# Rearranged heads in an encoder layer: map one is scaled earlier, products with v run their high passes first, GpSimd forms T1

## The chip, the core and the metric

The kernel runs on one core of a Trainium2 chip. Its engines work side by side and meet through semaphores: TensorE (PE: products, transposes), VectorE (DVE), ScalarE (ACT), GpSimd (POOL), and SyncE (SP), which issues most transfers. The metric is the time of one execution on the device in microseconds. The kernel before took 1401.86 us in the median of three runs (1399.14 to 1402.75).

## What is computed

One encoder layer for 1024 tokens of width 1024. Cut to what matters for the change, the token mixing is

```python
u = rmsnorm(h, norm_g[l, 0])
proj = u @ w_in            # q, k, v of 4 heads, inputs of a short convolution, gates
s1 = einsum('bhqd,bhkd->bhqk', q1b, k1) * scale + bias     # bias: ALiBi
s2 = einsum('bhqd,bhkd->bhqk', q2b, k2) * scale + bias
a = softmax(s1) - lam * softmax(s2)
o = einsum('bhqk,bhkv->bhqv', a, v)
o = rmsnorm(o, subln_g) * (1.0 - lam_init)
merged = g[:, :, 0] * y_conv + g[:, :, 1] * (o @ w_attn_out)
h = h + rmsnorm(merged @ w_o, norm_g[l, 1])
```

and after it comes an MLP with a squared ReLU of width 4096. A head has 64 columns for q1, q2, k1, k2 each and 128 for v.

## The kernel before

All products are made from operands split into a high and a low part (`_hi`, `_lo`): hi x hi, lo x hi and hi x lo, three passes for each of eight row tiles (`PASSES`), so 24 products of 128x128 by 128x512 for one unit. ScalarE writes the high part (a copy that rounds), VectorE the low part (the source less the high part).

The heads run as 4 x 8 **blocks** (i, n): head i, 128 query rows n. Every engine has its own list, written out by hand; all that joins them is semaphores. On TensorE block (i, n) is: `scores(i, n)`, both maps, 24 half-height products; one **unit** `filler(i, n)`, a product of 24 for another purpose; and `turn((i, "T", n - 1))`, eight transposes of the combined map of the block before. The fillers of head i are, for n = 0 to 7: v0, AV1 of the head before, v1, k0 and k1 of the next head, AV0 of this head, q0 and q1 of the next head. In head 3 the units at n = 3, 4, 6, 7 are gates (g0 to g3). AV is the product of the turned map (`at_hi`, `at_lo`) with v; AV0 takes the turned maps 0 to 3, AV1 those of 4 to 7. v is turned in the middle of unit n = 3 (`turn((i, "VT", 0))`). Units use two PSUM banks in turn, so one waits until the unit two before it is copied out.

For one block the other engines do this. VectorE: `maximum` for map two, then map one (bias added, the row maximum into `small`); ScalarE: `exponential` of each; VectorE: `weights`, the reciprocals of the sums and a weight for map two; GpSimd: `e1 * weight`, then `e0 + e1`; ScalarE between them: `first_scaled`, `e0` by its reciprocal. The sum is turned on TensorE one block later, and ScalarE and VectorE copy the turned tile into `at_hi` (`turned_hi`) and `at_lo` (`turned_lo`). Between these steps stand, at given n: the copies of q, k and v (`copy_hi`, `copy_lo`), the split of the next weight panel (`panel_hi`, `panel_lo`), and the norm of o: `av_copy`, `o_squares` (ScalarE), `o_squares_lo` (VectorE), `o_sum` (TensorE, two products with ones), `o_deviation` (ScalarE, a square root, with a load of its table before it and one of the exponential's behind it), `o_inverse` (VectorE, four reciprocals and the scaling).

`o_sum` is made inside an AV unit, halfway (`o_inside`), into the bank of the unit before; its values are read by `o_deviation`.

Behind the heads comes the GATE stage, a product in seven terms (X1, Y, X2, Z1, X3 and so on) on sums T1 to T4 of `act` halves, each split again. T1 is u12 - u11, 2048 elements in a partition, formed in three passes (`t_sum(GATE, 1, k)`, total `g_sum1`, hi and lo parts of both); T3 is formed in three passes within head 3 at n = 2, 4, 7; T2 needs T1, T4 needs T2. From there TensorE runs on through the branch products, w_o and the MLP.

Lines of before in the rows below: 927 the products of a unit, 974 the transposes of a turn, 1007 scores, 1067 GATE terms; 888 and 891 GpSimd's scale and sum; 1349 exponential, 1356 `first_scaled`, 1362 `turned_hi`; 1831 `turned_lo`, 1838 `panel_lo`, 1893 `copy_lo`, 1910 maximum, 1922 weights, 1946 and 1949 `o_inverse`, 1987 `t_sum`.

## Time and profile before

| | us |
|---|---|
| median of three runs | 1401.86 |
| the profiled execution | 1399.67 |
| its span, first to last instruction | 1397.8 |
| TensorE busy (97% of the span) | 1361.4 |
| VectorE busy (69%) | 965.6 |
| ScalarE busy (46%) | 643.9 |
| GpSimd busy (20%) | 284.5 |

Busy time counts the engines' own instructions; waiting and issuing transfers is not counted. Time and rows are all of this one execution. Matmuls overlap each other, so a mean duration is longer than the distance from one to the next. In the rows a number in square brackets is the idle time of the engine just before, with what ended it.

### The profile page before, as it was taken

The page shows a single profiled execution, that of the slowest core. Times are in us where ns is not written, and L with a number is a line of the kernel's source. Part 1 is how long each engine was busy: PE and PEld are TensorE (multiplying, and loading weights), DVE is VectorE, ACT ScalarE, POOL GpSimd, SP SyncE. Part 2 cuts the span into 40 slices and gives each one's busy share as a digit, 9 for nine tenths or more (in the row PEclk, how much of TensorE's full clock was granted, in tenths as well). Part 3 has the DMA queues.
Part 4 walks back from the last instruction along what each step waited for, and adds up shares of the span by engine and source line. Part 5 has one row for each costly group of instructions (what it writes and reads, how often), then busy time and mean ns, then how long its engine had stood idle before and what let it go on. Part 6 is the DMA issues. An engine that isn't in the chain of part 4 may idle for free.

```text
span 1397.8 us, 17130 instructions
## 1 busy us (share of the span) xinstructions
PE 1361.4 (97%) x6305; PEld 1113.8 (80%) x6305; DVE 965.6 (69%) x1423; ACT 643.9 (46%) x985; POOL 284.5 (20%) x136
## 2 busy tenths in 40 slices
PE   9999999998999999999999999999999999999998
PEld 7777767676788888888888888888888888888886
DVE  7567777777977754566556788766674787765676
ACT  7566776675622244521243453333332444444454
POOL 0465565664000000000000133333233100000000
PEclk9999999999999999999999999999999999999999
DMA  5110101001122233264642065444444974336343
GB/s 185 31 31 16 31 16 31 16 31 60 46 61 61 68 106 113 76 196 147 225 153 72 35 189 174 155 153 146 156 166 155 381 270 128 98 102 215 105 132 109
DMA packets 141656, 162.18 MB, mean 116 GB/s; under 512 B 6861, under 2 KB 88970, under 8 KB 141450
## 3 DMA queue, kind: packets, MB, share of 16 engines
q1 hardware_dynamic: 135568, 148.27, 33.0%
q10 hardware_dynamic: 6010, 12.88, 2.4%
q8 instruction: 48, 0.79, 0.2%
q14 instruction: 30, 0.25, 0.0%
HBM read 114.98 MB, written 46.14 MB: 115 GB/s over the span
## 4 chain that ended last, share of the span: by engine, by line
PE 83%; DVE 7%; issue 6%; ACT 4%; POOL 1%; ACTq 0%; DVEq 0%; POOLq 0%
PE psum L1067 35%; PE psum L1227 21%; PE psum L927 19%; PE psum L1204 3%; DVE dev L1946 1%; PE psum L1007 1%; DVE at_lo L1831 1%; ACT e L1349 1%; PE psum L974 1%; DVE g_sum L1987 1%; ACT at_hi L1362 1%; PE psum L936 1%; PE psum L1176 1%; ACT w_hi L1266 0%; ACT L1373 0%
## 5 line engine op out<-in xcount | busy, mean ns | idle before, releaser
L1227 PE MATMUL psum<-op 128*128 128x512 f32 x1344 | 305.1, 389 | 0.1
L1227 PEld LDWEIGHTS psum<-op 128*128 128x128 f32 x1344 | 252.2, 188 | 52.9 <-issue 0.5
L1693 ACT ACTIVATE op<-v 128x512 fp32r<-128x512 f32 x112 | 70.7, 632 | 151.0 <-PE psum L1227 147.9
L2403 DVE TENSOR_TENSOR op<-v,op 128x512 fp32r<-128x512 f32 x112 | 78.6, 702 | 88.3 <-ACT op L1693 88.3
L888 POOL TENSOR_SCALAR e<-e,small 128x1024 f32<-128x1024 f32 x32 | 95.1, 2973 | 140.1 <-DVE small L1924 140.1
L1349 ACT ACTIVATE e<-e,small 128x1024 f32<-128x1024 f32 x64 | 73.7, 1152 | 73.9 <-DVE small L1915 71.1
L927 PE MATMUL psum<-act_hi,w_hi 128*128 128x512 f32 x256 | 104.4, 408 | 0.9 <-DVE act_lo L1832 0.9
L927 PE MATMUL psum<-act_lo,w_hi 128*128 128x512 f32 x256 | 100.7, 393 | 0.0
L927 PE MATMUL psum<-act_hi,w_lo 128*128 128x512 f32 x256 | 100.7, 393 | 0.0
L1067 PE MATMUL psum<-act_hi,w_lo 128*128 128x512 f32 x256 | 99.6, 389 | 0.0
L1067 PE MATMUL psum<-act_hi,w_hi 128*128 128x512 f32 x256 | 99.6, 389 | 0.0
L1067 PE MATMUL psum<-act_lo,w_hi 128*128 128x512 f32 x256 | 99.6, 389 | 0.0
L894 POOL TENSOR_TENSOR staging<-w_raw 128x512 f32<-128x512 f32 x1 | 1.3, 1299 | 456.4 <-ACT w_raw L1630 456.4
L891 POOL TENSOR_TENSOR e<-e,e 128x1024 f32<-128x1024 f32 x32 | 81.6, 2551 | 18.1 <-ACT e L1356 16.7
L2406 DVE TENSOR_TENSOR op<-f_raw,op 128x512 fp32r<-128x512 f32 x112 | 77.7, 694 | 5.4 <-ACT op L1695 5.4
L1910 DVE CUSTOM_DVE_ANT_0 e<-psum,alibi 128x1024 f32<-128x1024 f32 x64 | 78.0, 1219 | 0.4 <-issue 0.3
L1695 ACT ACTIVATE op<-f_raw 128x512 fp32r<-128x512 f32 x112 | 69.0, 616 | 6.6 <-DMA f_raw<-f_scratch 6.6
L1438 ACT ACTIVATE prod<-psum 128x512 f32<-128x512 f32 x36 | 21.5, 597 | 104.9 <-PE psum L1067 80.3
L927 PEld LDWEIGHTS psum<-act_hi,w_hi 128*128 128x128 f32 x256 | 48.7, 190 | 20.2 <-issue 9.0
L927 PEld LDWEIGHTS psum<-act_hi,w_lo 128*128 128x128 f32 x256 | 48.5, 190 | 10.6
L1067 PEld LDWEIGHTS psum<-act_hi,w_hi 128*128 128x128 f32 x256 | 48.0, 188 | 10.0
L1067 PEld LDWEIGHTS psum<-act_hi,w_lo 128*128 128x128 f32 x256 | 48.1, 188 | 9.9
(271 smaller groups left out, 3158.0 us busy)
## 6 DMA issues: line engine op xcount, KB each, us to landing
f_raw<-f_scratch SPq DMA_DIRECT2D x112, 256.0 KB, 2.6
w_raw<-in_w_ff SPq DMA_DIRECT2D x32, 512.0 KB, 5.3
w_raw<-in_w_in SPq DMA_DIRECT2D x28, 512.0 KB, 4.5
f_scratch<-f_out SPq DMA_DIRECT2D x56, 256.0 KB, 2.3
v<-in_w_ff SPq DMA_DIRECT2D x12, 1024.0 KB, 7.0
gates_scratch<-staging ACTq DMA_DIRECT2D x32, 256.0 KB, 2.0
gate_in<-gates_scratch SPq DMA_DIRECT2D x16, 512.0 KB, 4.3
f_scratch<-staging SPq DMA_DIRECT2D x30, 256.0 KB, 2.2
```

Source lines behind the costliest of these rows:

```text
L888: nc.gpsimd.tensor_scalar(e[s][1][:], e[s][1][:], weight2[s], None, ALU.mult).then_inc(a_ready, 1)
L891: nc.gpsimd.tensor_tensor(e[s][0][:], e[s][0][:], e[s][1][:], ALU.add).then_inc(a_ready, 1)
L927: mm = nc.tensor.matmul(bank, stat(a, kt), moving(b, kt), start=(n == 0), stop=(n == len(terms) - 1))
L1067: mm = nc.tensor.matmul(bank, stat[a][:, kt], moving(b)[:, kt], start=(first and n == 0), stop=(last and n == len(terms) - 1), skip_group_ ...
L1204: mm = nc.tensor.matmul(bank, w_hl[panel % RING][a][:, kt], act_hl[b][:, kt, half_cols[h]], start=(kt == 0 and (a, b) == PASSES[0]), stop= ...
L1227: mm = nc.tensor.matmul(psum[:, (X_BANK, Z_BANK)[m % 2][t]], op[n % SLOTS][:, 2 + a, token_cols(t)], op[n % SLOTS][:, b], start=(m in (0, ...
L1349: nc.scalar.activation(e[s][c][:], e[s][c][:], ACT.Exp, scale=SCALE, bias=neg_max[s][:, c:c + 1], accum_out=exp_sum[s][:, c:c + 1]).then_i ...
L1693: nc.scalar.activation(op[n % SLOTS][:, 0], v_block[m][:, kt], ACT.Copy).then_inc(v_hi, 1)
L1695: nc.scalar.activation(op[n % SLOTS][:, 2], f_raw[:, n % SLOTS], ACT.Copy).then_inc(f_hi, 1)
L1910: vec.tensor_tensor_reduce(out=e[s][c][:], in0=psum[:, SB + 2 * c:SB + 2 * c + 2].rearrange("p b c -> p (b c)"), in1=table[:, start:start ...
L2403: vec.tensor_tensor(slot[:, 1], v_block[m][:, kt], slot[:, 0].bitcast(F32), ALU.subtract).then_inc(v_split, 1)
L2406: vec.tensor_tensor(slot[:, 3], f_raw[:, n % SLOTS], slot[:, 2].bitcast(F32), ALU.subtract).then_inc(f_split, 1)
```

## The change

It moves instructions and adds one small piece; no arithmetic is left out.

1. Scores of block (0,0) are issued in the middle of unit (0,q,1) instead of ahead of it.
2. A new function `av` makes the AV units: first all passes with `at_hi` (v high and v low, 16 products), then the eight with `at_lo`. It waits for `tb_hi` and for v's low part at the start, and for `tb_free` (`at_lo` written) only before the last eight.
3. `o_sum` is no longer made in AV units but in units n = 0 and n = 4 of the next head, for (3,0) in (3,7), by a table `O_IN`. `o_deviation` moves along to n = 0 and 4.
4. ScalarE: `first_scaled` stands first in a block, then `turned_hi`, then the copy. The first panel of a head is split at n = 2 instead of n = 0.
5. VectorE: `turned_lo` first; the low part of q or k behind the first maximum (n = 0, 4) or behind both; the reciprocals of o two by two, at the end of blocks 0 and 4 and ahead of the weights in blocks 1 and 5, the scaling behind these weights; the third panel at n = 6 instead of 5; the scaling of the bias table from n = 0 to n = 7.
6. GpSimd forms T1, three passes after its last sum of the heads; VectorE's three steps for it are gone. The tail of the heads on ScalarE and VectorE is ordered anew.

```diff
+O_IN = {filler(HEADS - 1, QB - 1): (HEADS - 1, 0)}
+for _i in range(1, HEADS):
+    O_IN[filler(_i, 0)] = (_i - 1, 0)
+    O_IN[filler(_i, 4)] = (_i - 1, 1)
...
+            pool.wait_ge(s_read, HEADS * QB)
+            for k in range(3):
+                pool.wait_ge(t_steps, GATE.t_sum_at(1) - 3 + k)
+                total = GATE.t_sums[1][:]
+                in0 = total if k else u_part(0, 1, 2).bitcast(F32)
+                in1 = (u_part(0, 1, 1), u_part(1, 1, 2), u_part(1, 1, 1))[k].bitcast(F32)
+                nc.gpsimd.tensor_tensor(total, in0, in1, ALU.add if k == 1 else ALU.subtract).then_inc(t_steps, 1)
...
+                def o_between():
+                    bank_read(BANKED[at - 1])
+                    o_sum(*O_IN[x])
...
+            def av(i, n):
+
+                at = BANK_AT[i, "AV", n]
+                if BANKED[at - 1] in O_IN:
+                    pe.wait_ge(o_read, half_at(*O_IN[BANKED[at - 1]]))
+                else:
+                    bank_read(BANKED[at - 2])
+                turned = TB_AT[i, "T", 4 * n + 3]
+                pe.wait_ge(tb_free, TB_AT[i, "VT", 0])
+                pe.wait_ge(tb_hi, turned)
+                terms = [(kt, a, 0) for kt in range(TT) for a in range(2)] + [(kt, 0, 1) for kt in range(TT)]
+                for k, (kt, a, b) in enumerate(terms):
+                    if k == 2 * TT:
+                        pe.wait_ge(tb_free, turned)
...
+                    if (i, n) == (0, 0):
+                        unit(x, (), lambda: scores(0, 0))
+                        continue
...
             def head(i):
                 for n in range(QB):
+                    if n > 0:
+                        first_scaled(i, n - 1)
+                    elif i > 0:
+                        first_scaled(i - 1, QB - 1)
+                    if n > 1:
+                        turned_hi((i, "T", n - 2))
...
-                        turned_lo((i, "T", n - 2))
-                    maximum(i, n, 1)
-                    maximum(i, n, 0)
...
+                    maximum(i, n, 1)
+                    if copied and n in (0, 4) and (i, n) != (0, 0):
+                        copy_lo(earlier)
+                    maximum(i, n, 0)
+                    if copied and n not in (0, 4):
+                        copy_lo(earlier)
...
+                    if n in (1, 5) and i > 0:
+                        for part in (2, 3):
+                            o_inverse(i - 1, n // 4, part)
...
+                    if n in (1, 5) and i > 0:
+                        o_scale(i - 1, n // 4)
+                    elif n in (0, 4) and i > 0:
+                        for part in range(2):
+                            o_inverse(i - 1, n // 4, part)
```

ScalarE from the panel split of block (1,3) to the exponentials of block (1,4), before: `e_0<-e_0` is the scaling of map one, `at_hi` the turned tile, `k_hi` the copy of k.

```order
L1266 ACTIVATE w_hi<-w_raw 128x1024
L1334 ACTIVATE k_hi<-psum 128x512
L1362 ACTIVATE at_hi<-psum 128x8x128
L1356 ACTIVATE e_0<-e_0,small 128x1024
L1349 ACTIVATE e_1,small<-e_1,small 128x1024
L1349 ACTIVATE e_0,small<-e_0,small 128x1024
```

The same place after, where the square root for o (`dev`) follows the exponentials:

```order
L1298 ACTIVATE w_hi<-w_raw 128x1024
L1388 ACTIVATE e_0<-e_0,small 128x1024
L1394 ACTIVATE at_hi<-psum 128x8x128
L1366 ACTIVATE k_hi<-psum 128x512
L1381 ACTIVATE e_1,small<-e_1,small 128x1024
L1381 ACTIVATE e_0,small<-e_0,small 128x1024
L1405 ACT_TABLE_LOAD
L1405 ACTIVATE dev<-psum,small 128x512
```

The scaling went from third to first behind the panel, the copy of k from first to third.

VectorE from the same panel to the second maximum of block (1,4), before: `small<-small 128x2` are the weights' reciprocals, `e_1` and `e_0` from psum the maxima.

```order
L1838 TENSOR_TENSOR w_lo<-w_raw,w_hi 128x1024
L1922 RECIPROCAL small<-small 128x2
L1924 TENSOR_SCALAR small<-small,par 128x1
L1893 TENSOR_TENSOR k_lo<-psum,k_hi 128x512
L1831 TENSOR_TENSOR at_lo<-psum,at_hi 128x8x128
L1907 MEMSET small 128x1
L1910 ISA e_1,small<-psum,alibi 128x1024
L1910 ISA small 128x1
L1915 TENSOR_SCALAR small<-small 128x1
```

and after:

```order
L1867 TENSOR_TENSOR w_lo<-w_raw,w_hi 128x1024
L1951 RECIPROCAL small<-small 128x2
L1953 TENSOR_SCALAR small<-small,par 128x1
L1860 TENSOR_TENSOR at_lo<-psum,at_hi 128x8x128
L1936 MEMSET small 128x1
L1939 ISA e_1,small<-psum,alibi 128x1024
L1939 ISA small 128x1
L1944 TENSOR_SCALAR small<-small 128x1
L1922 TENSOR_TENSOR k_lo<-psum,k_hi 128x512
```

The low part of k moved from ahead of the turned tile to behind the first maximum.

TensorE at the first AV unit, block (0,5), before: the last two passes of the scores, then the unit.

```order
L1007 MATMUL psum<-k_lo,q_hi 128x512 x4
L1007 MATMUL psum<-k_hi,q_lo 128x512 x4
L927 MATMUL psum<-at_hi,v_hi 128x512
L927 MATMUL psum<-at_lo,v_hi 128x512
L927 MATMUL psum<-at_hi,v_lo 128x512
```

and after, the end of the unit and what follows it:

```order
L1060 MATMUL psum<-at_hi,v_hi 128x512
L1060 MATMUL psum<-at_hi,v_lo 128x512
L1060 MATMUL psum<-at_lo,v_hi 128x512 x8
L982 MATMUL psum<-ident,e_0 128x128 x8
L1015 MATMUL psum<-k_hi,q_hi 128x512 x4
```

`at_lo` was read by the second product of the unit and is now read by its last eight.

## Rows read from the trace of the kernel before

**Rows 1.** The page, costliest groups: busy, mean ns, idle before.
```profile
L891 POOL TENSOR_TENSOR e<-e,e 128x1024 f32<-128x1024 f32 x32 | 81.6, 2551 | 18.1 <-ACT e L1356 16.7
```

**Rows 2.** TensorE's waits: engine, line, releaser, us in total, times, longest.
```profile
PE psum L927 <- DVE at_lo L1831: 11.1, 7, 2.9
PE psum L974 <- POOL e L891: 6.3, 4, 4.7
PE psum L1007 <- DVE small L1910: 3.2, 4, 0.8
PE psum L1007 <- DVE k_lo L1893: 2.8, 1, 2.8
```

**Rows 3.** Stretches: us, busy PE, PEld, DVE, ACT, POOL, clock, DMA share, GB/s.
```profile
104.42:178.21 73.79, 67.71 (x366) 52.66 (x365) 56.13 (x109) 50.47 (x66) 41.77 (x16) 1.00 0.08 22
178.21:252.24 74.03, 69.14 (x367) 53.86 (x366) 55.11 (x111) 51.75 (x69) 42.84 (x16) 0.98 0.08 22
252.24:338.24 86.00, 74.81 (x389) 58.20 (x388) 67.04 (x117) 58.61 (x76) 54.09 (x18) 0.98 0.12 36
...
37.98:41.39 3.41, 3.41 (x12) 2.25 (x9) 2.41 (x6) 0.95 (x1) 0.00 (x0) 0.50 0.55 156
```

**Rows 4.** TensorE in order of time: start, us, line, tiles, idle before.
```profile
36.83 0.73 PE L1007 MATMUL psum<-k_hi,q_hi 64*128 64x512 f32 x4 [2.82 <-DVE k_lo L1893]
...
88.14 0.73 PE L1007 MATMUL psum<-k_hi,q_hi 64*128 64x512 f32 x4
...
89.73 0.50 PE L927 MATMUL psum<-act_hi,w_hi 128*128 128x512 f32 x1
...
96.28 0.73 PE L1007 MATMUL psum<-k_hi,q_hi 64*128 64x512 f32 x4
...
115.77 0.47 PE L927 MATMUL psum<-at_hi,v_hi 128*128 128x512 f32 x1 [1.54 <-DVE at_lo L1831]
...
142.85 0.73 PE L1007 MATMUL psum<-k_hi,q_hi 64*128 64x512 f32 x4
...
338.24 1.91 PE L974 MATMUL psum<-ident,e 128*128 128x128 f32 x8 [4.74 <-POOL e L891]
...
377.22 0.47 PE L1067 MATMUL psum<-act_hi,g_S_hi 128*128 128x512 f32 x1 [1.25 <-issue]
```

**Rows 5.** VectorE in order of time: start, block (1,4), o's inverses, tail.
```profile
36.09 0.68 DVE L1893 TENSOR_TENSOR k_lo<-psum,k_hi 128x512 fp32r<-128x512 f32 x1
...
142.56 1.23 DVE L1838 TENSOR_TENSOR w_lo<-w_raw,w_hi 128x1024 fp32r<-128x1024 f32 x1 [0.85 <-ACT w_hi L1266]
143.71 0.16 DVE L1922 RECIPROCAL small<-small 128x2 f32<-128x2 f32 x1
...
144.03 0.68 DVE L1893 TENSOR_TENSOR k_lo<-psum,k_hi 128x512 fp32r<-128x512 f32 x1
144.63 1.21 DVE L1831 TENSOR_TENSOR at_lo<-psum,at_hi 128x1024 fp32r<-128x1024 f32 x1
...
149.84 0.17 DVE L1922 RECIPROCAL small<-small 128x2 f32<-128x2 f32 x1 [1.31 <-ACT e L1349]
...
311.17 1.71 DVE L1946 RECIPROCAL dev<-dev 128x128 f32<-128x128 f32 x2
312.91 2.10 DVE L1949 SCALAR_TENSOR_TENSOR o<-o,par,dev 128x512 f32<-128x512 f32 x1
...
353.79 0.75 DVE L1949 SCALAR_TENSOR_TENSOR o<-o,par,dev 128x512 f32<-128x512 f32 x1
...
355.06 2.28 DVE L1987 TENSOR_TENSOR g_sum<-act_hi,g_sum 128x2048 f32<-128x2048 f32 x1
```

**Rows 6.** ScalarE in order of time, block (1,4): the turned tile, the scaling.
```profile
142.96 1.03 ACT L1362 ACTIVATE at_hi<-psum 128x1024 fp32r<-128x1024 f32 x1
143.90 1.15 ACT L1356 ACTIVATE e<-e,small 128x1024 f32<-128x1024 f32 x1
```

**Rows 7.** GpSimd in order of time, block (3,7), beside a sum of VectorE.
```profile
329.08 4.82 POOL L888 TENSOR_SCALAR e<-e,small 128x1024 f32<-128x1024 f32 x1 [2.19 <-DVE small L1924]
```

More of the change, by code:

```diff
@@ L1026, in unit @@
                     pe.wait_ge(map1_read, HEADS * QB)
-                if kind == "AV":
-                    pe.wait_ge(tb_free, TB_AT[i, "T", 4 * n + 3])
-                    between = o_inside(x) and (lambda: (bank_read(before), o_sum(psum[:, 1 - at % 2], *o_inside(x))))
-                    product(unit_bank(x), lambda a, kt: v_hl[a][:, kt], lambda b, kt: at_hl[b][:, kt], range(TT), (),
-                            between).then_inc(proj_done, 1)
-                    return
+                def o_between():
+                    bank_read(BANKED[at - 1])
+                    o_sum(*O_IN[x])
                 panel = panel_of(x)
@@ L1055, in _ @@
             unit((HEADS, "g", 5))
-            unit((last, "AV", 1))
+            av(last, 1)
             unit((HEADS, "g", 6))
-            pe.wait_ge(o_read, half_at(last, 0))
-            o_sum(psum[:, 1 - BANK_AT[last, "AV", 1] % 2], last, 1)
+            bank_read((HEADS, "g", 3))
+            o_sum(last, 1)
             unit((HEADS, "g", 7))
@@ L1523, in _ @@
                 if p == GATE.first:
+                    t_hi_part(GATE, 4)
                     x_copy(GATE, 3, p)
@@ L2115, in _ @@
             panel_lo(P_BR - 1)
-            t_sum(GATE, 1, 0)
-            t_sum(GATE, 1, 1)
+            for part in range(2):
+                o_inverse(last, 0, part)
             turned_lo((last, "T", 7))
-            t_sum(GATE, 1, 2)
+            for part in range(2, 4):
+                o_inverse(last, 0, part)
+            o_scale(last, 0)
             t_lo(GATE, 3)
-            o_inverse(last, 0)
             av_copy(last, 1)
+            o_squares_lo(last, 1)
             t_sum(GATE, 2, 0)
-            o_squares_lo(last, 1)
             t_sum(GATE, 2, 1)
@@ L2184, in _ @@
                 if p == GATE.first + 2:
-                    o_inverse(HEADS - 1, 1)
-                if p == GATE.first:
-                    g_part_lo("W11", p + 1)
-                    g_part_lo("S4", p)
+                    for part in range(4):
+                        o_inverse(HEADS - 1, 1, part)
+                    o_scale(HEADS - 1, 1)
                 g_sum("S3", p + 1)
```

144 lines of the change are left out of this document (68 added, 76 removed).

## The prediction, made before the result was known

> **What bounds the kernel now.** I read the list of TensorE's waits first, then the busy time by head, then TensorE's own rows at the waits, and last one block's rows on VectorE and ScalarE. TensorE is the bound, and from 377 us on nothing makes it wait before the last microseconds. All that can be won lies ahead of that. The list [rows 2] shows which waits: 11.1 us in seven waits of the product with v for `at_lo`, 6.3 us in four waits of a turn for GpSimd's sum, 3.2 us of scores for a maximum, 2.8 us once for `k_lo`. The busy time by head [rows 3] says the same: 73.79 us with 67.71 busy, 74.03 with 69.14, 86.00 with 74.81. After an idle stretch of 2.8 us or more the granted clock is 0.50 for 3.41 us (1.2 instead of 2.4 GHz), which costs half of it, 1.7 us [rows 3]; the head of 74.03 us and the 86.00 have the other ones. After the 1.54 us at 115.77 it did not fall [rows 4]. A plain block lasts 8.14 us on TensorE (88.14 to 96.28), 1.59 of it scores [rows 4].
>
> **Part 1, the start.** Scores (0,0) wait 2.82 us for `k_lo`, which VectorE ends at 36.77 [rows 5], and the clock falls behind it [rows 3, 4]. After the change the first half of unit (0,q,1), 12 of 24 products or 2.8 us, stands ahead of them; TensorE is free from 34.0 and reaches the scores at about 36.7, when `k_lo` is done. Both costs go: 2.8 + 1.7 = 4.5, less 0.1 of rest: **-4.4 us**. The cover is those 12 products; they need only panel 1 and the copy of (0,q,0), both long there.
>
> **Part 2, what the product with v waits for.** It now needs `at_hi` at its start and `at_lo` 16 products (3.6 us) later. `at_lo` takes 1.21 us [rows 5], so that wait is covered. But `at_hi` comes later than before: ScalarE now scales map one (`e_0`, 1.15 us [rows 6]) ahead of it, and that waits for the weights of the block before. This closes a loop that was open: weights(n-1), scaling, `at_hi`, `at_lo`, maxima, exponentials, weights(n). Its length from rows: 143.71 to 143.90 is 0.19; scaling 1.15; `at_hi` 1.03 [rows 6]; from `at_lo`'s start to the next weights 149.84 - 144.63 = 5.21 [rows 5]; with 0.03 between, **7.6 us against a block's 8.14**. Only 0.5 us is spare, so whatever stands in the loop makes a lag that hardly drains. In it stand the q/k copy between the maxima at n = 0 and 4 (0.68), a panel's low part ahead of the weights at n = 2 and 3 (1.23 behind ScalarE's high part of about 1, so some 2.2), the turn of v at n = 3, and the inverses at n = 1 and 5 (1.71 for two [rows 5], mostly in the 1.4 us that VectorE waits for the second exponential).
>
> **Part 3, o's sums in another unit.** They move into units (i,v,0) and (i+1,k,1), and at the midpoint TensorE waits for the copy of the unit before, whose low part VectorE makes behind the first maximum. Block n = 4 worked out from the start of its scores: weights(3) at +1.05 (before: 143.71 - 142.85 = +0.86 [rows 4, 5]), then 0.19 + 1.15 + 1.03 + 0.03 to `at_lo`, 1.15 to the maximum, 1.34 for it, 0.68 for `k_lo`: +6.6. TensorE is at its midpoint at 1.59 + 2.8 = +4.4. So this wait is new: **2.2 to 2.3 us**. Queued behind it are o's sum, half a unit and turn 3.
>
> **Sum of a head.** I carried the three orders forward with the pitches of rows 4 to 6. Waits of head 1: 1.0 at n = 0 (o's sum), 1.05 at n = 1 (`at_hi`), 1.25 at n = 3 (turn 2, for v's low part), 2.3 at n = 4, 1.05 at n = 5 (`at_hi`): 6.65. The work is 8 x 8.14 + 0.9 for v's turn + 0.9 for two sums = 66.9. Together 73.5 against 73.79 and 74.03 [rows 3]: **-0.8 us** for heads 1 and 2, so nearly all the wait removed from the product with v comes back elsewhere. Head 0 gets worse: no wait for o there, so the lag of n = 3 and 4 comes out at n = 5, 1.9 us where about 1 was, and 0.5 in two turns: **+1.4**. Head 3 has no q/k copies, but T3's sums (2.28 each [rows 5]) stand behind the weights. Carried forward to the last turn, which was at 338.24 [rows 4], it comes at 333.4, 4.9 earlier; of this 3.8 is from the terms above, so **-1.1**. Two microseconds of this are GpSimd's last sum, which no longer waits for T1.
>
> **Part 4, T1 on GpSimd.** Three passes of 2048 elements; the trace of before has only 1024 at a mean of 2.55 us [rows 1], so 4.8 to 5.1 each, 14.4 and more, from 333.3 on. VectorE and GpSimd kept each other out here: scaling o took 2.10 us beside a GpSimd sum and 0.75 alone, and a GpSimd pass took 4.82 beside a sum of VectorE [rows 5, 7]. In the tail o's scaling (0.75) and T3's low part (2.28) fall between the passes and wait for them; so T1 ends at about 348.4 and the copy of the last o stands at 350.7, where it stood behind o's scaling at 353.79 + 0.75 = 354.5, just ahead of T2's sum at 355.06 [rows 5]. T2 needs T1 then: met. From there the chain is as long as before but for 0.5 that ScalarE's last gate with its table load adds: X3 started at 377.22 [rows 4], now at about 372.8. **+0.5**. Bounds of a pass: at 2.28, VectorE's own time for this size, T1 would be done 7 us sooner and the last o copied when its product ends, 3 us sooner; at 8 it is the third rival. I take the rate of the 1024 rows, the nearest.
>
> The Trainium skill (SBUF — State Buffer, Who interferes with whom) calls this an exclusive lock, held for a whole instruction by whoever issued first, and so speaks against long GpSimd passes in the tail. The two rows agree with it; each VectorE pass with two SBUF operands would wait up to a full GpSimd pass, which the sum takes from rows and the third rival carries to its end.
>
> **Sum.** -4.4 + 1.4 - 0.8 - 1.1 + 0.5 = **-4.4 us**. The profiled execution took 1399.67 us (span 1397.8), so 1395.3 for it; the median of the runs is 2.2 us above that execution, at 1401.86, and 1401.86 - 4.4 = 1397.5. One place is open to either side: in block (3,5) T3's second sum and GpSimd's add are 0.1 us apart; if VectorE is first, 2.2 us more are won. The forecast is -2.5 to -7, point **1397.4**.
>
> **Rivals.**
> First, the lag drains (more won). If the extras in the loop fit, since VectorE has gaps where I put it busy, the 2.3 at n = 4 of heads 1 and 2 and the other order in (3,5) are won: -4.4 - 4.6 - 1.0 = -10, **1392**. For it: before, the weights came as late as +0.86 and the next block had recovered [rows 5]. Against it: before, the scaling stood outside the loop.
> Second, nothing to be measured. My waits of 1.9, 2.3, 2.3, 2.6 and 2.8 us lie between 1.54 (no fall of the clock) and 2.8 (fall). Each fall costs 1.7, of which the lag gives about half back, since the loop catches up meanwhile: 5 x 0.8 = +4, **1401.4**. The same time comes out if the change is only reordered waits beyond the start.
> Third, slower. GpSimd's T1 holds VectorE's tail. The copy of the last o is reached earlier than before only if three passes and the 3.0 us between them end before about 354.5, that is in 21 us from 333.3; the decisive pass length is 6 us. At 8 us a pass: 24 + 3 = 27, the copy at 360.3, 5.9 later than before: **1407.8**. For it: a pass over twice the elements has no row. Against it: 2.55 per 1024 [rows 1].
>
> **How the numbers follow.** Forecast 0.54, first rival 0.16, second 0.22, third 0.08. About 0.3% is what a measurement of this kernel can tell from no change, here 4.2 us, or 1397.7. The forecast lies across it, a little more on the fast side (0.34 of 0.54); with the first rival 0.50 for faster. Within 0.3%: 0.20 + 0.22 = 0.42. Slower 0.08. The range takes the forecast with both ends, the first rival and the second: 1392 to 1402.
>
> **What would show it.** Right: scores (0,0) inside (0,q,1) with no wait and full clock at 38; the products with v wait for `at_hi`, about 1 us each, and never for `at_lo`; a new wait of o's sum for `k_lo` of about 2 us in blocks (1,4) and (2,4) and for `q_lo` of 1 us in (1,0), (2,0); heads of 73 to 74 us; three GpSimd passes of about 5 us behind the last add; X3 near 373. Wrong: no such waits of o's sum (then the first rival), rows at clock 0.50 in the middle of heads 1 and 2 (the second), or GpSimd passes of 6 us and more with T2's sum behind them (the third).

## The result: 1390.83 us, and the profile after

The changed kernel took **1390.83 us** in the median (1390.60 to 1391.22, 4 runs), the kernel before beside it 1400.50 (1399.10 to 1402.75, 4 runs). The ratio is 0.9935, with a 95% interval from 0.9919 to 0.9951. The profiled span went from 1397.8 to 1388.5 us. The forecast was 1397.4, the range ended at 1392, and the time lies outside it. The sum said 4.4 us; 9.7 were won against the kernel before run beside it, and 11.0 against the 1401.86 that the forecast started from.

TensorE's waits in the changed kernel, in the form of [rows 2]. The line numbers of the changed kernel are: 935 a unit (927 before), 982 the turn, 1001 o's sum, 1060 the product with v, 1099 the GATE terms.

```profile
PE psum L1060 <- ACT at_hi L1394: 7.1, 7, 2.2
PE psum L1001 <- DVE k_lo L1922: 3.5, 2, 1.8
PE psum L982 <- POOL e L891: 2.5, 1, 2.5
PE psum L982 <- DVE v_lo L1860: 2.0, 3, 1.0
PE psum L1099 <- ACT prod L1470: 2.0, 1, 2.0
...
PE psum L1001 <- DVE o_squares L1970: 1.1, 1, 1.1
```

The product with v no longer waits for `at_lo` but seven times for `at_hi`; o's sum waits for `k_lo` in two heads; the start's wait for `k_lo` is gone. The prediction named all of these. One that it named, of o's sum for `q_lo` at n = 0, is not in the list, and the sizes differ. The heads 1, 2 and 3, as in [rows 3]:

```profile
100.76:172.22 71.46, 67.74 (x365) 52.66 (x365) 52.66 (x111) 51.28 (x69) 42.96 (x17) 1.00 0.08 23
172.22:243.92 71.70, 67.84 (x365) 52.67 (x364) 52.65 (x111) 51.52 (x69) 43.20 (x17) 1.00 0.08 23
243.92:326.30 82.38, 75.58 (x391) 58.51 (x391) 61.81 (x112) 58.32 (x76) 52.30 (x19) 0.98 0.07 23
```

Head 1 has 71.46 us where it had 73.79, head 2 71.70 where it had 74.03, the last one 82.38 where it had 86.00. TensorE's rows at the places that the prediction spoke of, as in [rows 4]:

```profile
36.65 0.50 PE L1015 MATMUL psum<-k_hi,q_hi 64*128 64x512 f32 x2
...
111.95 0.47 PE L1060 MATMUL psum<-at_hi,v_hi 128*128 128x512 f32 x1 [0.71 <-ACT at_hi L1394]
...
142.76 0.50 PE L1001 MATMUL psum<-o_squares,ones 128*128 128x512 f32 x1 [1.76 <-DVE k_lo L1922]
...
326.30 0.33 PE L982 MATMUL psum<-ident,e 128*128 128x128 f32 x1 [2.54 <-POOL e L891]
...
360.63 0.47 PE L1099 MATMUL psum<-g_t_hi,g_S_hi 128*128 128x512 f32 x1 [1.99 <-ACT prod L1470]
...
367.79 0.39 PE L1099 MATMUL psum<-act_hi,g_S_hi 128*128 128x512 f32 x1
```

The last of these is X3, at 377.22 before. The same by stages, in us; "last turn" is the last transposing of a map, and the forecast is the prediction's term:

| stretch | before | after | change | forecast |
|---|---|---|---|---|
| to scores (0,1) | 45.62 | 41.20 | -4.4 | -4.4 |
| to head 1 | 58.80 | 59.56 | +0.8 | +1.4 |
| heads 1 and 2 | 147.82 | 143.16 | -4.7 | -0.8 |
| head 3 to the last turn | 86.00 | 82.38 | -3.6 | -1.1 |
| last turn to X3 | 38.98 | 41.49 | +2.5 | +0.5 |
| sum | | | -9.4 | -4.4 |

What the sum missed lies in the third and fourth line, and the last one goes the other way.

### The profile page after: what moved, and what is told of

It is laid out like the page before. It is cut to its first block, busy times and chain, and to the rows that moved or that the text cites. A ratio compares the mean times of both kernels' runs of the same rounds, so it can differ in the third digit from the quotient of the medians.

```text
span 1388.5 us, 17131 instructions
## 1 busy us (share of the span) xinstructions
PE 1360.8 (98%) x6305; PEld 1112.4 (80%) x6305; DVE 961.7 (69%) x1420; ACT 642.8 (46%) x985; POOL 298.5 (21%) x139
## 4 chain that ended last, share of the span: by engine, by line
PE 76%; ACT 8%; issue 8%; DVE 8%; DMA 1%; POOL 0%; SPq 0%; DVEq 0%; ACTq 0%
PE psum L1099 35%; PE psum L1259 22%; PE psum L935 15%; PE psum L1236 3%; ACT e L1388 2%; ACT at_hi L1394 2%; ACT e L1381 2%; DVE dev L1975 1%; DVE w_lo L1867 1%; ACT L1405 1%; ACT w_hi L1298 1%; DVE small L1944 1%; DMA w_raw<-in_w_in 1%; PE psum L1208 1%; DVE g_t_lo L2028 0%
## 5 line engine op out<-in xcount | busy, mean ns | idle before, releaser
L888 POOL TENSOR_SCALAR e<-e,small 128x1024 f32<-128x1024 f32 x32 | 98.9, 3090 | 144.7 <-DVE small L1953 144.7
L891 POOL TENSOR_TENSOR e<-e,e 128x1024 f32<-128x1024 f32 x32 | 76.8, 2400 | 2.7
L1860 DVE TENSOR_TENSOR at_lo<-psum,at_hi 128x1024 fp32r<-128x1024 f32 x32 | 39.2, 1224 | 36.9 <-ACT at_hi L1394 36.9
L935 PEld LDWEIGHTS psum<-act_hi,w_lo 128*128 128x128 f32 x256 | 48.4, 189 | 10.5
```

The source lines that it names most:

```text
L888: nc.gpsimd.tensor_scalar(e[s][1][:], e[s][1][:], weight2[s], None, ALU.mult).then_inc(a_ready, 1)
L891: nc.gpsimd.tensor_tensor(e[s][0][:], e[s][0][:], e[s][1][:], ALU.add).then_inc(a_ready, 1)
L935: mm = nc.tensor.matmul(bank, stat(a, kt), moving(b, kt), start=(n == 0), stop=(n == len(terms) - 1))
```

## The loop from weights to weights

The prediction said that the scaling of map one, now ahead of the turned tile, closes a loop: the weights of one block release, through ScalarE and VectorE, the weights of the next. It can be read in the changed kernel in a plain block, (3,4) to (3,5). First VectorE: the weights, the tile's low part, the next weights.

```profile
281.45 0.16 DVE L1951 RECIPROCAL small<-small 128x2 f32<-128x2 f32 x1
...
283.74 1.22 DVE L1860 TENSOR_TENSOR at_lo<-psum,at_hi 128x1024 fp32r<-128x1024 f32 x1 [1.88 <-ACT at_hi L1394]
...
288.95 0.17 DVE L1951 RECIPROCAL small<-small 128x2 f32<-128x2 f32 x1 [1.31 <-ACT e L1381]
```

Then ScalarE between them: the scaling, which waited 1.37 us for these weights, and the tile right behind it.

```profile
281.64 1.15 ACT L1388 ACTIVATE e<-e,small 128x1024 f32<-128x1024 f32 x1 [1.37 <-DVE small L1951]
282.70 1.00 ACT L1394 ACTIVATE at_hi<-psum 128x1024 fp32r<-128x1024 f32 x1
```

From start to start: 0.19 + 1.06 + 1.04 + 5.21 = 7.50 us. Now follow the same instruction, the weights of n = 0, from head 1 to 2 to 3:

```profile
107.89 0.17 DVE L1951 RECIPROCAL small<-small 128x2 f32<-128x2 f32 x1 [1.31 <-ACT e L1381]
...
179.58 0.17 DVE L1951 RECIPROCAL small<-small 128x2 f32<-128x2 f32 x1 [1.31 <-ACT e L1381]
...
251.27 0.17 DVE L1951 RECIPROCAL small<-small 128x2 f32<-128x2 f32 x1 [1.31 <-ACT e L1381]
```

Twice 71.69 us. The eight distances from weights to weights in head 1 are 9.44, 9.63, 10.29, 8.11, 10.04, 7.79, 8.29 and 8.10. TensorE's own work in a head is 67.1 us (below), so the head lasts as long as the loop, and TensorE waits for the rest, 4.4 us. The list of waits says the same from the other side: in heads 1 and 2 (100.76 to 243.92) no wait of VectorE or ScalarE is ended by TensorE; they wait for each other alone, VectorE 17.1 us for `at_hi` and ScalarE 33.9 us for the maxima. A new theory came out of this: **in the changed kernel the loop with all that stands in it is the bound of heads 1 and 2, not TensorE**. The rival was that there is no such loop, and that every wait is local, won or lost by the order in one block.

## Experiments on the start and on the product with v

All times are medians; the ratio is that to the kernel before, run beside.

**start_only**: the kernel before with part 1 alone.

```diff
+                    if (i, n) == (0, 0):
+                        unit(filler(0, 0), (), lambda: scores(0, 0))
+                        continue
```

> The kernel before with one edit: the scores of block (0,0) stand in the middle of unit (0,q,1). The first term of the sum by itself. Loop theory (the start is worth its 4.4 us, and the heads' own share of the measured 9.1 is 4 to 5 us because the closed loop takes the rest back): -4.4 us, block (0,1) starts 4.4 us earlier, at 41.2, and every later block too. Rival (the start is mostly given back in head 0, since the other engines cannot follow): under -2.5 us at the start of head 1 (104.42 before).

Measured: 1396.81 us (1395.15 to 1399.15), ratio 0.998 [0.997, 0.9991], which is 1.3 to 4.2 us. The profiled spans differ by 4.0 (1393.8 against 1397.8), the medians by 2.9 (1399.76 beside it). In the trace every block up to the product with v of (2,1) comes 4.2 us earlier (186.90 against 191.14), and the term is there; in the time somewhat less than 4.4 is left.

**high_first_only**: the kernel before with the new order of passes in AV units, o's sum still in their middle.

```diff
+                    terms = [(kt, a, 0) for kt in range(TT) for a in range(2)] + [(kt, 0, 1) for kt in range(TT)]
...
+                        if k == 2 * TT:
+                            pe.wait_ge(tb_free, turned)
```

> The kernel before with the product with v in the new order (16 products with at_hi, then 8 with at_lo), o's sum still in its middle, all other lists as before. at_hi was complete 1.2 us before at_lo, so of the seven waits (11.1 us) about 3.2 should be left, and the two falls of the clock behind them (1.7 each) go. Loop theory: the scaling still stands behind at_hi, no loop is closed, so most of this stays: -7 to -9 us, more than the heads of the changed kernel gained by all their edits (about 5). Rival, the lists' order is what pays: the waits move to the scores' and the turns' waits, and less than 4 us is left.

Measured: 1398.98 us, ratio 0.9986 [0.9976, 0.9996]; span 1397.1, 0.7 less. TensorE's waits, to be held against [rows 2]:

```profile
PE psum L1007 <- DVE small L1919: 6.5, 6, 1.3
PE psum L974 <- POOL e L891: 6.3, 4, 4.7
PE psum L974 <- DVE at_lo L1840: 5.0, 6, 2.5
PE psum L1038 <- ACT at_hi L1371: 3.4, 3, 1.6
```

The loop theory expected far more and failed here; its rival held. The 11.1 us of waits in the product with v became 3.4, but the wait of scores for the maxima rose from 3.2 to 6.5 and that of turns for `at_lo` to 5.0. With the old lists of ScalarE and VectorE, a wait taken from TensorE in one place comes back as a wait further on.

**start_and_high_first**: both edits in the kernel before.

> The two edits above together in the kernel before. Loop theory: the sum of the two, -11 to -13 us, so 1388 to 1390, as fast as the changed kernel or faster without any of its new lists. Rival: the new lists are worth 2 us and more, so this is slower than the changed kernel's 1390.8, at 1393 or above.

Measured: 1395.33 us, ratio 0.9971 [0.9959, 0.9984]; span 1393.2. The rival held again: the rest of the change is worth another 4.5 us.

## Experiments on the loop

**scaling_second**: the changed kernel, ScalarE copies the turned tile first and scales second.

```diff
-                    if n > 0:
-                        first_scaled(i, n - 1)
-                    elif i > 0:
-                        first_scaled(i - 1, QB - 1)
                     if n > 1:
                         turned_hi((i, "T", n - 2))
                     elif i > 0:
                         turned_hi((i - 1, "T", 6 + n))
+                    if n > 0:
+                        first_scaled(i, n - 1)
+                    elif i > 0:
+                        first_scaled(i - 1, QB - 1)
```

> The changed kernel, in which ScalarE copies the turned tile's high part first and scales map one behind it, as the kernel before did; everything else as changed. What it tells: whether the scaling ahead of the turned tile closes a loop that costs. Loop theory (the one of the prediction, its length now 7.5 us from the trace of the changed kernel instead of 7.6): with the tile first the loop is opened and the tile is 1.06 us earlier, so the waits of the product with v for at_hi (7.1 us in seven) fall below 2 and o's sum waits for k_lo some 1 us less each time: 2 to 4 us faster than the changed kernel, 1387 to 1389. Rival (the scaling first pays): GpSimd's two passes begin behind the scaling, so the sum for the turn comes 1.06 us later in every block whose turn is tight, (3,5) and the last turn above all, which waited 2.3 and 2.7 us for GpSimd or the tile: these grow to 3.4 and 3.7 us, and VT and other turns begin to wait: 0 to 3 us slower, 1391 to 1394.

Measured: **1373.24 us** (1373.20 to 1373.31), ratio 0.9804 [0.9778, 0.9831]: 17.6 us less than the changed kernel. The loop theory had the sign and gave 2 to 4; its rival expected a loss. Heads 1 and 2 and the last one to its last turn:

```profile
99.35:166.44 67.09, 67.09 (x365) 52.69 (x365) 52.10 (x111) 51.57 (x68) 43.82 (x17) 1.00 0.09 24
166.44:233.55 67.11, 67.11 (x365) 52.69 (x364) 52.07 (x111) 51.55 (x68) 43.82 (x17) 1.00 0.08 24
233.55:309.18 75.63, 73.53 (x392) 57.36 (x391) 59.66 (x112) 58.91 (x76) 52.96 (x19) 1.00 0.08 25
```

TensorE is busy for all of 67.09 us: no wait for `at_hi`, none for `k_lo`, none for v in heads 1 and 2. Every wait of these heads went when one instruction no longer stood first, and now ScalarE waits for turns of TensorE (five times in head 1, 4.4 us), so TensorE leads. My own expectation (2 to 4 us) was too small since it counted two kinds of waits only, and only where they showed in the list.

**scaling_in_pieces**: a dose. The changed kernel, the scaling in four instructions of 256 columns.

```diff
-                nc.scalar.activation(e[s][0][:], e[s][0][:], ACT.Copy, scale=recip[s][:, 0:1]).then_inc(exp_done, 1)
+                for k in range(4):
+                    cols = slice(k * part, (k + 1) * part)
+                    scaled = nc.scalar.activation(e[s][0][:, cols], e[s][0][:, cols], ACT.Copy,
+                                                  scale=recip[s][:, 0:1])
+                scaled.then_inc(exp_done, 1)
```

> The changed kernel, in which ScalarE scales map one in four pieces of 256 columns instead of one of 1024, the signal behind the last. A dose in the loop: some 0.4 to 0.5 us more in each block (1.15 for 1024 columns, 0.63 for 512, so about 0.37 for 256). The loop from weights to weights, 7.50 us in a plain block, becomes 7.9 to 8.0 against TensorE's 8.14, so its spare falls from 0.64 to 0.2. Loop theory: what the k and q copies (0.6 each, four to a head), v's turn and the panels put into it no longer drains; 1.5 to 3 us more in each of heads 1 to 3 and 1 in head 0: 1396 to 1401. Rival (no loop; the waits come from single blocks' order): each place waits at most 0.45 us longer, 9 places: 1391 to 1394.

Measured: 1404.23 us (1403.77 to 1404.86), ratio 1.0026 [1.0013, 1.0039], 13.4 us more than the changed kernel. The weights of n = 0 in heads 1 and 2:

```profile
111.78 0.17 DVE L1956 RECIPROCAL small<-small 128x2 f32<-128x2 f32 x1 [1.31 <-ACT e L1381]
...
187.83 0.17 DVE L1956 RECIPROCAL small<-small 128x2 f32<-128x2 f32 x1 [1.31 <-ACT e L1381]
```

76.05 us instead of 71.69: 4.36 more, 0.47 to 0.57 in each of the eight blocks, and a plain block, (3,4) to (3,5), went from 7.50 to 8.07. All of the dose appears in the head's time although a plain block is still shorter than TensorE's 8.14. That is what a loop does that bounds the head as a whole. The rival (0.45 at nine places, at most 1394) is out; the loop theory's own 1396 to 1401 was too low, since it gave a head 1.5 to 3 us and 4.36 came.

**pieces_scaling_second**: the control, the same pieces behind the tile.

> The kernel with the scaling second (1373.24), in which the scaling is made in four pieces as in the run with pieces, where 0.56 us a block more made the changed kernel 13.4 us slower. Control for the dose. Loop theory: the weights no longer stand behind a scaling of the block before that stands ahead of the tile, so 0.56 us more of ScalarE's work a block falls into its idle time: 1373 to 1375 (0.5 us at the last turn, which waits for GpSimd behind the scaling). Rival (ScalarE or GpSimd is simply short of time): 8 to 14 us slower, 1381 to 1387.

Measured: 1373.32 us (1373.12 to 1373.53), ratio 0.9809 [0.9785, 0.9833]: 0.1 more than with the scaling second. The same work costs 13.4 us inside the loop and nothing outside it.

**scaling_first_in_before**: the kernel before with `first_scaled` first in each block, nothing else.

> The kernel before, in which ScalarE scales map one first in each block, ahead of the copy and the turned tile: this step of the change alone. Loop theory: it closes the loop in a kernel whose product with v waits for the tile's low part, so the lag falls on TensorE in full: the 11.1 us of that wait grow by 1.1 us at each of seven places and waits for maxima appear; 6 to 15 us slower than before, 1406 to 1415. Rival (the scaling first helps GpSimd, whose sums are then earlier, and the 4.7 us wait at the last turn shrinks): 1398 to 1401.

Measured: 1430.82 us, ratio 1.0217 [1.0189, 1.0244], 31 us slower than before, over twice the expected upper end.

```profile
PE psum L927 <- DVE at_lo L1831: 31.4, 7, 6.0
PE psum L1007 <- DVE small L1910: 6.8, 6, 2.5
```

The wait for `at_lo` went from 11.1 to 31.4 us. So this step is a loss in either kernel.

## Experiments on the other lists

**k_copy_first**: the changed kernel, at n = 4 both parts of k's copy first (`copy_hi` ahead of `first_scaled`, `copy_lo` ahead of `turned_lo`).

> The changed kernel, in which at n = 4 of heads 0 to 2 both parts of the copy of k stand first on ScalarE and VectorE, ahead of the scaling and the turned tile. What it tells: whether the new wait of o's sum for k_lo (3.5 us in two waits, 1.92 in block (1,4)) is lost time, or whether it only holds back what would wait behind it. Theory 'a wait is a cost': it goes, and 2 x 1.9 us are won, 1387. Theory 'the lag is one and shows at the next gate': the tile of n = 4 comes 0.9 us later on ScalarE and 0.68 later on VectorE, so the product with v at n = 5, which waited 1.62, 0.87 and about 0.9 us for at_hi in the three heads, waits 1.5 to 2.5 us; of 3.8 us at most 1 is won: 1390 to 1391.

Measured: 1389.89 us (1389.83 to 1391.52), ratio 0.9923 [0.9896, 0.995]: 0.9 less than the changed kernel, as the second theory said.

```profile
PE psum L1060 <- ACT at_hi L1394: 9.5, 7, 2.2
PE psum L982 <- POOL e L891: 2.8, 2, 2.6
PE psum L982 <- DVE v_lo L1863: 2.1, 3, 1.0
```

The 3.5 us of o's sum for `k_lo` are gone and the wait for `at_hi` grew from 7.1 to 9.5. Where a loop is the bound, it matters little at which place TensorE waits for it.

**inverses_together**: the changed kernel, o's four reciprocals in one piece with the scaling, behind the weights of n = 1 and 5.

```diff
-                    if n in (1, 5) and i > 0:
-                        for part in (2, 3):
-                            o_inverse(i - 1, n // 4, part)
...
                     if n in (1, 5) and i > 0:
+                        for part in range(4):
+                            o_inverse(i - 1, n // 4, part)
                         o_scale(i - 1, n // 4)
-                    elif n in (0, 4) and i > 0:
-                        for part in range(2):
-                            o_inverse(i - 1, n // 4, part)
```

> The changed kernel, in which the four reciprocals for o stand in one piece behind the weights of blocks 1 and 5, with the scaling, instead of two at the end of blocks 0 and 4 and two ahead of the weights. What it tells: the worth of spreading them. The four take 4 x 0.86 = 3.4 us. Theory 'spreading pays': VectorE has gaps of 1.3 to 1.4 us at each weights, which the spread pairs fill; in one piece they push the tile's low part and the maxima of blocks 2 and 6 back by about 2 us, which exceeds the 0.6 us spare in a block, so scores or turns of blocks 2 and 3, 6 and 7 wait: 1 to 2 us for each of six places less what drains, 1394 to 1398. Theory 'the gap is anyway there': VectorE is idle 31% of the span, and a block later it is level again: within 1 us of the changed kernel, 1390 to 1392.

Measured: 1408.06 us (1407.54 to 1409.06), ratio 1.0054 [1.0038, 1.0069]: 17.2 us more than the changed kernel, more than the first theory said. Heads 1 and 2:

```profile
100.86:177.56 76.70, 68.42 (x365) 52.51 (x364) 55.15 (x109) 50.03 (x67) 41.83 (x16) 1.00 0.07 21
177.56:256.63 79.07, 70.01 (x364) 53.65 (x364) 56.44 (x112) 51.54 (x69) 42.23 (x16) 0.98 0.07 21
```

**inverses_together_open**: the same edit on the kernel with the scaling second.

> The kernel with the scaling second, and the four reciprocals of o in one piece behind the weights of blocks 1 and 5 (this second edit cost 17.2 us on the changed kernel, where the loop is closed). Loop theory: 17.2 us came from the loop, in which 1.7 us ahead of the maxima come round again block after block; with the loop open (7.5 us of chain cut at the scaling) VectorE has 8.14 - 5.7 = 2.4 us free in a block, and 3.4 us together are caught up within two blocks: at most 0.7 us at each of six places, 1373 to 1377. Rival (the lists' balance pays by itself, loop or not): about the same 17 us, 1388 to 1391.

Measured: 1379.38 us (1379.08 to 1379.54), ratio 0.9848 [0.9822, 0.9874]: 6.1 us, a third of the 17.2, though more than the loop theory's upper end. Both are at work: 11.1 of the 17.2 us need the closed loop, and 6.1 are lost even where it is open.

**av_waits_for_all_open**: the scaling second, and the product with v waits for `at_lo` at its start.

```diff
-                pe.wait_ge(tb_hi, turned)
+                pe.wait_ge(tb_free, turned)
```

> The kernel with the scaling second, in which the product with v, its passes in the new order, waits for the tile's low part at its start instead of ahead of its last eight products. What it tells: what the high passes first are worth where the loop is open. In the trace with the scaling second the product of block (1,1) starts at 109.60 and the low part ends at 111.18: 1.6 us at each of seven such places, and the wait moves the rest of the block with it, so nothing is caught up: 7 x 1.6 = 11 us more, 1384. Rival (the low part comes earlier once TensorE waits, as the lag drains): 3 us or less, 1376. On the kernel before the same step alone gained 0.8 us.

Measured: 1387.88 us (1386.56 to 1388.18), ratio 0.991 [0.9886, 0.9935]: 14.6 us more than with the high passes first.

```profile
PE psum L1060 <- DVE at_lo L1860: 12.4, 7, 3.3
```

The step that gained 0.7 to 0.8 us on the kernel before is worth 14.6 once the lists let it.

**copies_first_open**: the changed kernel with copy, tile, scaling on ScalarE and the low part of k or q first on VectorE, as before the change.

> The changed kernel with the copy of k, q or v first, the turned tile second and the scaling third on ScalarE, and the low part of k or q first on VectorE: the order of the kernel before for these, all else as changed. The loop is open in it as well. The tile's high part comes 0.6 to 0.7 us later than with the tile first, at 109.9 instead of 109.23 in block (1,1), the product with v starts at 109.60: 0.3 us at each of seven places, 0.6 where the copy is late: 2 to 4 us more than 1373.24, 1375 to 1377. Rival (the order of the copies is where the other lists' gain came from): 1385 or more.

Measured: 1375.73 us (1374.75 to 1376.48), ratio 0.9824 [0.98, 0.9849]: 2.5 more than with the scaling second, within the range but not by the seven waits that it was added up from. In its trace heads 1 and 2 have no wait at all; the product with v waits 2.34 us once, in block (3,5), and the granted clock is about half for 3.4 us behind it.

**panels_old_open** and **table_at_0_open**: the scaling second, and the weight panels split at the old n, or the bias table scaled at n = 0 again.

> The kernel with the scaling second (1373.24), with the weight panels split where the kernel before split them: the first at n = 0 instead of 2 and, on VectorE, the third at n = 5 instead of 6. A low part is 1.23 us and stands ahead of the weights; at n = 0 and 5 it meets the low part of q or k (0.68) and a pair of inverses (1.8), so 3.7 us beyond the plain 5.7 in a block of 8.14: 1.3 us over, at two blocks of each of three heads, if nothing is caught up: 3 x 2 x 1.3 = 8 us, 1381. Rival (caught up in the next block, whose spare is 2.4 us, before TensorE asks): within 1.5 us, 1372 to 1375.

> The kernel with the scaling second (1373.24), with the bias table's scaling (1024 columns, about 0.6 to 1.2 us on VectorE) back ahead of the maxima of block n = 0, instead of behind those of n = 7. It pushes the maxima and the weights of three blocks by its length, in a block that also holds a copy and two inverses. If nothing is caught up: 3 x 1 = 3 us, 1376. Rival: caught up, within 1 us, 1373 to 1374.

Measured: 1377.97 us (ratio 0.983 [0.981, 0.9851]) and 1377.15 (0.9823 [0.9802, 0.9843]): 4.7 and 3.9 more by the medians, 3.6 and 2.7 by the ratios, whose intervals overlap with that of scaling_second (the kernel before took 1402.02 beside them, 1399.52 beside scaling_second). The traces show the cost itself, so neither delay was caught up in full: in the first, in each of heads 1 to 3, a product with v waits 0.63 to 0.65 us and a turn behind it 0.31 to 0.34; in the second o's sum waits 0.96 for `q_lo`, three times.

So of the 22.1 us between start_and_high_first (1395.33) and scaling_second (1373.24), four list edits, each undone alone, account for 6.1 + 4.7 + 3.9 + 2.5 = 17.2 by the medians and some 15 by the ratios; whether they add is not known. The place of o's sum and the order of the lists in the tail were not tried alone.

## Experiments on the tail

**t1_on_vector**: the changed kernel with T1's three passes on VectorE.

```diff
-            pool.wait_ge(s_read, HEADS * QB)
-            for k in range(3):
-                pool.wait_ge(t_steps, GATE.t_sum_at(1) - 3 + k)
...
+            t_sum(GATE, 1, 0)
+            t_sum(GATE, 1, 1)
             for part in range(2):
                 o_inverse(last, 0, part)
             turned_lo((last, "T", 7))
+            t_sum(GATE, 1, 2)
```

> The changed kernel with T1 formed by VectorE again, its three passes where they stood. By the prediction's term: GpSimd's last sum waits for two of these passes again, the last turn 1.8 to 2 us later, but VectorE's tail no longer waits for GpSimd's passes (the trace after shows o's scaling at 5.1 instead of 0.75 and T3's low part at 6.7 instead of 2.3). If the lock in the tail costs as much as T1's move saves: within 1.5 us of the changed kernel. If the move is the gain: 3 us and more slower than it.

Measured: 1388.54 us (1388.47 to 1388.74), ratio 0.9919 [0.9903, 0.9936]: 2.3 less than the changed kernel, and neither expectation. VectorE in the tail of the changed kernel, o's scaling, T3's low part and the last o's copy, with GpSimd's passes behind:

```profile
331.91 5.11 DVE L1980 SCALAR_TENSOR_TENSOR o<-o,par,dev 128x512 f32<-128x512 f32 x1
336.95 6.68 DVE L2028 TENSOR_TENSOR g_t_lo<-g_sum,g_t_hi 128x2048 fp32r<-128x2048 f32 x1
343.56 0.68 DVE L1965 TENSOR_SCALAR o<-psum 128x512 f32<-128x512 f32 x1
```

```profile
326.20 5.57 POOL L899 TENSOR_TENSOR g_sum<-act_hi 128x2048 f32<-128x2048 f32 x1
331.85 9.63 POOL L899 TENSOR_TENSOR g_sum<-g_sum,act_lo 128x2048 f32<-128x2048 f32 x2
```

And with T1 on VectorE:

```profile
338.99 0.75 DVE L1972 SCALAR_TENSOR_TENSOR o<-o,par,dev 128x512 f32<-128x512 f32 x1
339.66 2.28 DVE L2023 TENSOR_TENSOR g_t_lo<-g_sum,g_t_hi 128x2048 fp32r<-128x2048 f32 x1
341.86 0.69 DVE L1957 TENSOR_SCALAR o<-psum 128x512 f32<-128x512 f32 x1
```

The move took 3 x 2.28 = 6.8 us off VectorE and lengthened two of its instructions by 4.4 + 4.4 = 8.8. The second and third pass of GpSimd run from 331.85 to 336.47 and from 336.56 to 341.49. The two instructions, issued just behind their starts, end 0.55 and 2.14 us after the passes, about their own 0.75 and 2.28: each stood still until the pass was over and only then ran. The copy of the last o comes 1.7 us later with T1 on GpSimd, and so does X2 (360.63 against 358.96). By the end of the profiled executions 1.6 us of it are left.

**x1_copy_first**: the changed kernel, X1's first slice copied ahead of the last gate on ScalarE.

> The changed kernel, in which ScalarE copies X1's first slice ahead of the last gate (with its table load) instead of behind it. In the trace of the changed kernel X2 waits 2.15 us at 360.6 for that copy, and the granted clock is 0.50 for 3.4 us behind it. Theory: both are a cost of ScalarE's order alone: X2 starts 1.3 us or more earlier (the table load is 1.28 and the gate about 1), the wait is under 1.0 us and the clock doesn't fall: 1.3 + 1.7 = 3 us faster, 1387.8. Rival: X2 or X3 then waits for a term of T2 or T4 instead, which stood just behind: half of it or less is won, 1389.5 or more.

Measured: 1390.71 us (1390.61 to 1390.85), ratio 0.9929 [0.9902, 0.9956], 0.1 less: the rival. X2's 2.0 us wait for the copy went, and two of 0.7 (for `g_S_lo` and `w_lo`) and one of 1.4 at a later term (379.07) came.

**scaling_second_t1_vector**: both gains in one kernel.

> The changed kernel with the tile's high part ahead of the scaling of map one (which alone took 1373.24) and with T1's three passes back on VectorE (which alone took 1388.54, 2.3 us less than the changed kernel). What it tells: whether the two gains add. In the trace with the scaling second, o's sum waits 2.91 us at 329.4 for the squares of the last o, since its copy stands behind T3's low part, 6.7 us long beside GpSimd's pass; the product itself ended at 321.2. Theory (the lock in the tail costs, wherever the tail begins): with T1 on VectorE this wait goes and nothing replaces it: 2.3 to 2.9 us less, 1370.5. Rival (the tail is now early enough that VectorE's three extra passes, 6.9 us, come late for T2): T2's terms wait, no gain: 1373 or more.

Measured: **1371.08 us** (1370.91 to 1371.20), ratio 0.9789 [0.9763, 0.9815]; 2.2 less than with the scaling second alone, as the theory said, though not with nothing in its place: the wait for the squares fell from 2.75 to 0.57, and X2's grew from 0.91 to 2.00. This beats both kernels, the changed one by 19.8 us. X1's early copy on top (open_t1_x1):

> The kernel with the scaling second and T1 on VectorE (1371.08), with X1's first slice copied ahead of the last gate. There X2 waits 2.16 us at 341.3 for that copy, behind the gate's table load and the gate. The same edit gained nothing on the changed kernel: X2's wait for the copy went, 0.7 us for w_lo and 0.7 for g_S_lo came in its place. Theory: the same here, 0 to 0.8 us less, 1370.3 to 1371. Rival: VectorE is 2 us earlier without GpSimd's passes, so 1.5 us or more are won, 1369.5 or less.

Measured: 1371.26 us, ratio 0.9795 [0.9771, 0.9819]: no difference.

## Why the prediction was wrong

**The start** (part 1) was right: -4.4 forecast, -4.4 in the trace at the scores of (0,1). The run with this part alone gave 4.0 by the spans and 2.9 by the medians.

**The product with v and the loop** (part 2) was right in kind and, for a plain block, in size: 7.6 forecast, 7.50 found. But "a lag that hardly drains", against a spare of 0.5 us a block, was the wrong way to work on from there. With its extras the loop is longer than TensorE's head (71.7 against 67.1), so no lag comes and goes: the head's time is the sum of the loop's eight distances. I should have added those. The prediction's list of what stands in the loop also lacked o's square root with its table load, behind which ScalarE's scaling waited in block (1,1):

```profile
107.87 1.28 ACT L1405 ACT_TABLE_LOAD   x1
109.17 0.69 ACT L1405 ACTIVATE dev<-psum,small 128x512 f32<-128x512 f32 x1
109.75 1.14 ACT L1388 ACTIVATE e<-e,small 128x1024 f32<-128x1024 f32 x1
```

**The step that failed is "Sum of a head".** The five waits of head 1 were to be 1.0, 1.05, 1.25, 2.3 and 1.05, together 6.65. Held block by block against the kernel with the scaling second, in which nothing waits here, the trace has 0.14 at n = 0, 0.78 at n = 1, 0.73 at n = 3, 1.98 at n = 4 and 0.75 at n = 5: 4.4. The work was 66.9 forecast, 67.1 found. All five were oversized, together by 2.3 us. One reason is in the rows: I laid durations end to end, while instructions in a row on one engine start 0.1 us closer than the first lasts (1.15 long, 1.06 to the next). By my estimate that is 0.1 in each of eight blocks (7.6 against 7.50), 0.8 of the 2.3. For the rest I only argue a reason: I counted the copies and panels in full where VectorE waits 1.31 us for the second exponential anyway. Heads 1 and 2 gave -4.7 instead of -0.8. In head 3 -1.1 became -3.6; how far the same waits made this was not taken apart. There the product with v of block (3,5) did wait 2.15 us for `at_hi`, and T3's second sum did stand behind GpSimd's add (292.63, 4.27 us long): the race went the way that I took.

**"Nearly all the wait comes back elsewhere"** was true of the kernel that I did not look at: of the high passes first on the old lists, which gained 0.7 us. In the changed kernel the heads brought 7.5 of the 9.4 us. Two large effects stand against each other in it: 17.6 us lost by the scaling in front, and more than that won by the other lists and the high passes. I costed the other lists (inverses spread, panels and bias table moved) at nothing of their own; with the loop open they are worth 6.1, 4.7 and 3.9 by the medians.

**Head 0** was +0.8 where +1.4 was forecast, again by sizes: the wait at (0,5) was 1.5 and not 1.9 (the block took 9.65 us, a plain one 8.14), and the 0.5 in two turns did not come.

**The tail** (part 4) had the right mechanism, and nearly the right price of a pass, 5.57, 4.62 and 4.93 against 4.8 to 5.1. From the first pass to the copy of the last o it had 350.7 - 333.3 = 17.4 us, and measured are 343.56 - 326.20 = 17.4. Its sum was +0.5, measured is +2.5: X2 waited 2.0 us for the copy of X1 behind the last gate, the clock fell behind it (1.7) and o's sum waited 1.13 where it had waited 0.32, while the 1.25 at X3 [rows 4] went away. The run with T1 on VectorE puts the price of the move at 2.3.

**The rivals.** The first gave 1392 and is the nearest, but that is luck: it had the 2.3 at n = 4 disappear and VectorE win the race in (3,5); 2.0 stayed, and GpSimd was first. The second had a part of its mechanism right and failed by its sum. For its five waits (1.9, 2.3, 2.3, 2.6 and 2.8), taken in order of time, the trace has 1.45, 1.76, 1.77, 2.15 and 2.54. The first three left the clock at full, and heads 1 and 2 stand at 1.00; behind the last two it fell to 0.50 for 3.41 us each (from 293.40 and 327.53), below the 2.8 of the prediction. With the one at X2 that makes three falls, where the kernel before had four, so no loss came of it. The third was far off, no pass reached 6 us. In the tail the trace agrees with the exclusive lock that the prediction cited from the Trainium skill (SBUF — State Buffer, Who interferes with whom): 0.75 became 5.11 and 2.28 became 6.68.

What stays open is how much of the 9.4 us each list edit brings in the changed kernel itself, with its closed loop. Of the list edits only the inverses (17.2 us lost) and, at n = 4, the place of k's copy (0.9 won) were undone there.

## What to carry to other kernels

When several engines run fixed lists, look for a loop that goes from an instruction through the others back to its next copy, and add up all distances of one period with everything that stands in it; if that sum exceeds the bounding engine's work, the loop is the bound, and each instruction in it counts in full. A move that puts a late result's consumer ahead of an early one's on the same engine closes such a loop: test that swap alone, in the new kernel and in the old one. And the worth of one step depends on the rest: the same order of passes was worth 0.7 us on one set of lists and 14.6 on another.

## What was not expected of the hardware

**The fall of the clock does not follow from the length of the wait.** The kernel before and start_only have the same wait at block (2,1). In the kernel before the matmuls behind it slow down at once (the granted clock is 0.50 for 3.41 us from 191.58 on):

```profile
191.14 0.47 PE L927 MATMUL psum<-at_hi,v_hi 128*128 128x512 f32 x1 [2.87 <-DVE at_lo L1831]
191.45 0.51 PE L927 MATMUL psum<-at_lo,v_hi 128*128 128x512 f32 x1
191.76 0.63 PE L927 MATMUL psum<-at_hi,v_lo 128*128 128x512 f32 x1
```

In start_only they do not, after 2.90 us:

```profile
186.90 0.47 PE L927 MATMUL psum<-at_hi,v_hi 128*128 128x512 f32 x1 [2.90 <-DVE at_lo L1834]
187.21 0.39 PE L927 MATMUL psum<-at_lo,v_hi 128*128 128x512 f32 x1
187.44 0.40 PE L927 MATMUL psum<-at_hi,v_lo 128*128 128x512 f32 x1
```

In the changed kernel the wait of 1.99 at 360.63 brought a fall (the clock is the last number but two):

```profile
361.66:365.07 3.41, 3.41 (x10) 2.63 (x9) 3.41 (x4) 0.00 (x0) 0.00 (x0) 0.50 0.72 204
```

With the scaling second and T1 on VectorE a wait of 2.00 at the same place did not; the clock stays at 1.00 up to 360:

```profile
341.26 0.47 PE L1091 MATMUL psum<-g_t_hi,g_S_hi 128*128 128x512 f32 x1 [2.00 <-ACT prod L1462]
```

So a wait of 2 to 3 us in a trace has a price of 1.7 us more only sometimes, and the prediction's "2.8 us or more" was no rule.
